# Turning softmax tiles by key blocks from the last one, a sink column, and decay terms on the row halves of the scores

## The chip, the cores and the metric

One core of a Trainium2 chip runs the whole program. The metric is device time in microseconds (us). TensorE (PE in the profile) multiplies, VectorE (DVE) and ScalarE (ACT) work on its results, GpSimd (POOL) takes elementwise work and issues some DMAs, SyncE (SP) issues the loads of weights. Each engine runs its own instructions in order, and they wait for each other on semaphores. A measurement of this kernel can tell about 0.2% from no change.

## What is computed

512 tokens of width 1024 pass through a model of two blocks. The first has two layers; each is an FFN, a mixer and another FFN. The second has a layer with differential attention, one with forgetting attention, and a convolutional FFN after each. Three kinds of stage hold attention, and each of them has eight slots, one for each pair of heads (or of softmaxes):

```
# mixer ("mix_0", "mix_1"), heads 0 to 7: window of 128 keys, and a sink in the denominator
m = max(max(s), sink);  p = exp(s - m);  denom = sum(p) + exp(sink - m);  o = (p / denom) @ v
# mixer, heads 8 to 11 (blocks) and 12 to 15 (scores of an index decide on 128 keys of a row)
# differential attention ("diff"), per head: two softmaxes over 64 channels each
attn = softmax(q1 k1 + b) - lam * softmax(q2 k2 + b);  o = attn @ v
# forgetting attention ("fox"), 16 heads: c is the running sum of the log forget gates
logits = q k / 8 + c[t] - c[s];  p = softmax(logits over s <= t);  o = p @ v
```

Everything is float32. Large products are made in three passes of TensorE with high and low parts (`h_hi`, `h_lo`, `w_hi`, `w_lo`).

## The kernel before

Tokens are split into four query tiles of 128 (i = 0 to 3) and four key blocks of 128 (b = 0 to 3). Tile i sees i + 1 blocks, or two of them for the windowed heads (`narrow`). `pair_plan` makes a plan for each pair p of heads. Its `phases` say in which of three parts of a slot the scores of a tile are made, last tile first: tile 3; then 2 and 0; then 1 (narrow: 3 and 2; then 1 and 0).

A slot is written out by hand in `pair_slots`, for each engine, and has three parts. In part `part` of slot p, TensorE makes the scores of pair p + 1 for the tiles of that phase (`pair_scores`), turns a share of the softmax tiles of pair p by transposes into two banks in turn (`pair_turn`), and then fills with a projection (`gemm_blocks`, nine matmuls of 512 columns, six in part 2). After part 2 it multiplies the turned tiles of pair p by the values (`pair_values`). VectorE does scores plus bias, with a running minimum (`pair_max`, line 1505), the reciprocal of the row sums (`pair_sums`), part of the scaling by it (line 1537), and other work between them: in the mixer rounds of a top-k (`rounds`, lines 1466 and 1467), elsewhere the low half of the next weights (line 1223). ScalarE does the exponentials (`pair_exps`, line 974), the copies of turned tiles out of the banks (`pair_turned` of ScalarE, line 993; VectorE's share is line 1550), and the high half of the next weights (line 772). GpSimd, in the mixer, makes the low half of the next weights (`low`, line 683) and then scales all tiles of the first six pairs (`pair_scale`, line 676); of the last two pairs of the mixer and of fox it scales tiles 0 and 1, and VectorE tiles 2 and 3.

What is turned together is a step: a head x of the pair and a group n of key blocks. Before the change a step with key block 0 comes first, and key block 0 is seen by every tile. So the first transposes of a head wait until all its tiles are scaled (`pn_ready` from GpSimd, `pl_ready` from VectorE), and the steps of head 0 come ahead of those of head 1.

For windowed heads the sink goes its own way: VectorE adds minimum and sink (line 1515), ScalarE takes the exponential (line 981), VectorE adds it to the row sums (line 1527) ahead of the reciprocal (line 1528).

In fox the decay is two more terms of the sum over channels. Its high and low parts, and ones, stand in four rows of `decay_q` and `decay_k` for each head, at partition 32 * (h % 4), and line 2065 adds them to the scores by a matmul of 4 rows. The scores themselves (line 2056) are matmuls of 64 rows, head 0 of a pair on rows 0 to 63 and head 1 on rows 64 to 127. GpSimd prepares both tensors and brings the rows in with 64 DMAs.

## Time and profile before

| what | value |
|---|---|
| median of 3 runs | 3302.03 us |
| lowest and highest | 3300.53 and 3302.58 us |
| profiled execution | 3302.81 us |
| its span | 3301.0 us |
| its mean granted clock of TensorE | 0.986 of 2.4 GHz |
| TensorE busy | 3190.7 us (97%) |
| VectorE, ScalarE, GpSimd busy | 1780.7, 1160.3, 548.0 us |
| stretches with attention slots | 459 to 594, 1421 to 1556, 2055 to 2190 and 2719 to 2861 us |

The profile is one execution. Times are from the start of the span. A row of the timeline has the start, the duration, the engine, the line of the kernel, the instruction, and what it writes and reads; "x6" joins six instructions. What stands in brackets is the idle time of the engine ahead of it and what ended it. Matmuls overlap, so the distance between two starts tells more than the duration.

### The profile page before, as it was taken

What the parts mean: (1) busy time and instruction counts of PE and PEld (TensorE: products, weight loads), DVE (VectorE), ACT (ScalarE), POOL (GpSimd) and SP (SyncE); (2) the same over time, 40 slices, a digit from 0 to 9 for tenths busy, and PEclk for the clock granted to TensorE, in tenths of its full rate; (3) what the DMA queues carried; (4) which work ended last, traced back from release to release, by engine and by line L of the source; (5) the groups of instructions that cost most, each with busy time, mean ns of one, the idle gap of its engine ahead of it and who ended that gap; (6) DMA issues with size and microseconds to landing.
All of it is one profiled execution on the core that took longest, in us unless ns stands there. A gap on an engine that the chain in (4) does not pass through costs nothing.

```text
span 3301.0 us, 42533 instructions
## 1 busy us (share of the span) xinstructions
PE 3190.7 (97%) x14834; PEld 2560.7 (78%) x14834; DVE 1780.7 (54%) x2737; ACT 1160.3 (35%) x1894; POOL 548.0 (17%) x506
## 2 busy tenths in 40 slices
PE   8999998999999999988999999989999999999998
PEld 7788765788888888765888877667888886688887
DVE  4434487543445344585543454557656555576474
ACT  4323235322223222344322232534324335344242
POOL 0000335300020000254100030231000432310003
PEclk9999999999999999999999999999999999999998
DMA  4355321233333333211333323112333231123332
GB/s 123 97 141 145 105 83 33 77 98 93 96 101 96 102 89 106 76 52 39 91 108 87 105 73 115 39 58 70 105 92 99 73 91 39 52 70 101 95 97 76
DMA packets 541547, 287.99 MB, mean 87 GB/s; under 512 B 14532, under 2 KB 537511, under 8 KB 541441
## 3 DMA queue, kind: packets, MB, share of 16 engines
q1 hardware_dynamic: 535936, 273.32, 28.7%
q0 software_dynamic: 5504, 13.31, 1.4%
q8 instruction: 61, 1.00, 0.1%
q14 instruction: 46, 0.37, 0.0%
HBM read 284.30 MB, written 10.02 MB: 89 GB/s over the span
## 4 chain that ended last, share of the span: by engine, by line
PE 83%; DVE 8%; POOL 4%; issue 2%; ACT 2%; DMA 0%; DVEq 0%; ACTq 0%; POOLq 0%
PE bank L1818 69%; PE bank L1832 4%; PE bank L2056 2%; PE bank L1849 2%; PE bank L1912 1%; PE bank L2097 1%; PE bank L2120 1%; POOL probs L676 1%; DVE w_lo L1223 1%; DVE norm_t L1308 1%; ACT w_hi L772 1%; POOL probs_mix L676 1%; PE bank L1890 1%; DVE score L1467 0%; POOL decay_q L741 0%
## 5 line engine op out<-in xcount | busy, mean ns | idle before, releaser
L772 ACT ACTIVATE w_hi<-w_raw 128x1024 fp32r<-128x1024 f32 (+2 forms) x477 | 533.2, 1119 | 1425.0 <-PE bank L1818 786.7
L1818 PE MATMUL bank<-h_hi,w_hi 128*128 128x512 f32 x2548 | 1000.8, 393 | 6.9 <-DVE h_lo L1248 3.8
L1818 PE MATMUL bank<-h_hi,w_lo 128*128 128x512 f32 x2548 | 992.4, 389 | 0.0
L1818 PE MATMUL bank<-h_lo,w_hi 128*128 128x512 f32 x2536 | 987.5, 389 | 0.0
L1223 DVE TENSOR_TENSOR w_lo<-w_raw,w_hi 128x1024 fp32r<-128x1024 f32 (+1 forms) x445 | 618.9, 1392 | 462.0 <-ACT w_hi L772 461.9
L1818 PEld LDWEIGHTS bank<-h_hi,w_hi 128*128 128x128 f32 x2548 | 477.8, 188 | 119.0 <-issue 14.5
L1818 PEld LDWEIGHTS bank<-h_hi,w_lo 128*128 128x128 f32 x2548 | 477.7, 187 | 101.0
L1818 PEld LDWEIGHTS bank<-h_lo,w_hi 128*128 128x128 f32 x2536 | 475.8, 188 | 100.1 <-issue 1.9
L1818 PE MATMUL bank<-act_hi,w_hi 128*128 128x512 f32 x924 | 360.6, 390 | 0.0
L1818 PE MATMUL bank<-act_lo,w_hi 128*128 128x512 f32 x924 | 360.4, 390 | 0.0
L1818 PE MATMUL bank<-act_hi,w_lo 128*128 128x512 f32 x924 | 360.3, 390 | 0.0
L1818 PEld LDWEIGHTS bank<-act_hi,w_hi 128*128 128x128 f32 x924 | 174.1, 188 | 36.6 <-issue 0.4
L1818 PEld LDWEIGHTS bank<-act_hi,w_lo 128*128 128x128 f32 x924 | 174.0, 188 | 36.3
L1818 PEld LDWEIGHTS bank<-act_lo,w_hi 128*128 128x128 f32 x924 | 174.0, 188 | 36.2
L1338 DVE SCALAR_TENSOR_TENSOR xres<-bank,xres 128x512 f32 (+1 forms) x64 | 44.2, 691 | 248.6 <-PE bank L1818 248.5
L1323 DVE TENSOR_TENSOR scaled_g<-bank,rstd 128x512 f32<-128x512 f32 x132 | 91.2, 691 | 150.6 <-PE bank L1818 145.7
L625 POOL TENSOR_TENSOR ssq<-xres 128x512 f32<-128x512 f32 x6 | 6.2, 1040 | 967.8 <-DVE xres L1338 945.8
L889 ACT ACTIVATE gated<-scaled_g 128x512 f32<-128x512 f32 x88 | 55.6, 632 | 298.3 <-DVE scaled_g L1323 298.2
L628 POOL TENSOR_TENSOR ssq<-ssq,psq 128x512 f32<-128x512 f32 x62 | 137.6, 2219 | 4.8
L1323 DVE TENSOR_TENSOR proj<-bank,rstd 128x512 f32<-128x512 f32 (+1 forms) x84 | 57.3, 686 | 109.6 <-PE bank L1818 109.2
L1379 DVE TENSOR_TENSOR prod<-gate_r,bank 128x512 f32<-128x512 f32 x88 | 60.5, 687 | 99.1 <-PE bank L1818 99.0
L683 POOL TENSOR_TENSOR w_lo<-w_raw,w_hi 128x1024 fp32r<-128x1024 f32 x32 | 77.0, 2405 | 214.0 <-ACT w_hi L772 214.0
(321 smaller groups left out, 3973.9 us busy)
## 6 DMA issues: line engine op xcount, KB each, us to landing
w_raw<-in_ffn_w_gate_dram SPq DMA_DIRECT2D x88, 512.0 KB, 3.8
w_raw<-in_ffn_w_up_dram SPq DMA_DIRECT2D x88, 512.0 KB, 3.8
w_raw<-in_ffn_w_down_dram SPq DMA_DIRECT2D x64, 704.0 KB, 4.5
w_raw<-in_ffn_w_in_dram SPq DMA_DIRECT2D x88, 512.0 KB, 3.8
w_raw<-in_ffn_w_out_dram SPq DMA_DIRECT2D x32, 704.0 KB, 4.5
w_raw<-in_w_in_dram SPq DMA_DIRECT2D x34, 512.0 KB, 3.8
w_raw<-in_a_w_qkv_dram SPq DMA_DIRECT2D x24, 512.0 KB, 3.8
w_raw<-in_w_out_dram SPq DMA_DIRECT2D x16, 512.0 KB, 3.5
```

The costliest lines, as they stand in the source:

```text
L628: add = nc.gpsimd.tensor_tensor(ssq[:, :], ssq[:, :], psq[:, :], ALU.add)
L676: ins = nc.gpsimd.tensor_scalar(tile, tile, recip[:, g % 4, i:i + 1], None, ALU.mult)
L683: nc.gpsimd.tensor_tensor(w_lo[c % 2][:, 0:KT, :], raw[c % 2][:, 0:KT, :], w_hi[c % 2][:, 0:KT, :].bitcast(f32), ALU.subtract).then_inc(lo ...
L772: nc.scalar.activation(w_hi[c % 2][:, 0:nk, 0:cols], raw[c % 2][:, 0:nk, 0:cols], ACT.Copy).then_inc(hi_ready, 1)
L889: nc.scalar.activation(gated[:, :], scaled_g[:, :], ACT.Silu).then_inc(silu_ready, 1)
L1223: nc.vector.tensor_tensor(w_lo[c % 2][:, 0:nk, 0:cols], raw[c % 2][:, 0:nk, 0:cols], w_hi[c % 2][:, 0:nk, 0:cols].bitcast(f32), ALU.subtra ...
L1323: nc.vector.tensor_tensor(dst, result(c)[rows, :], rstd[rows, :], ALU.mult).then_inc(bank_free[c % 2], 1)
L1379: nc.vector.tensor_tensor(prod[:, :], gate_r[:, :], result(at + 1)[:, :], ALU.mult).then_inc(bank_free[(c + 1) % 2], 1)
L1818: mm = nc.tensor.matmul(result(c)[0:cols, :], w[b][:, k, 0:cols], x[k], start=(k == 0 and n == 0), stop=(k == nk - 1 and n == 2))
L1832: mm = nc.tensor.matmul(bank[c % 2][:, :], w[c % 2][:, k, :], x[k], start=(k == 0 and n == 0), stop=(k == KT - 1 and n == 2))
L1849: mm = nc.tensor.matmul(result(u)[:, :], w[u % 2][:, k, :], x[k], start=(k == 0 and n == 0), stop=(k == nk - 1 and n == 2))
L2056: mm = nc.tensor.matmul(PAIR_S[x][:, at:at + w], job["q"][:, P * i:P * (i + 1)], job["k"][:, first:first + w], start=True, stop=alone)
```

## The change

- **Steps by key blocks, from the last.** Groups are now key blocks 2 and 3, then 0, then 1 (narrow: 2 and 3, then 0 and 1). Outside the differential stage both heads' steps of a group stand together, so part 0 turns group 0 of both heads, part 1 group 1, part 2 group 2. A step waits only for the tiles that it reads. In the differential stage the upper tiles are announced apart from the lower ones. The number of transposes stays the same.
- **The sink as a column.** The biased scores of windowed heads get one more column, filled with minus the sink by a copy on VectorE ahead of each `pair_max` instruction; the exponential covers it and its row sum holds the sink. Lines 1515, 981 and 1527 go.
- **Decay on the row halves.** `decay_q` now has, on the 64 rows of each half, four rows for each of the eight pairs; `decay_k` has eight copies, zero outside the four rows of their pair. The decay matmul takes the same 64 rows as the scores. GpSimd fills `decay_k` by a copy of 4096 columns where it had a memset of 2048, `decay_q` by a memset of 512 where it had 2048, makes `causal` after the gates are ready (in the place of `rms`), and issues 36 DMAs where it had 64.

The rest of the diff replaces `off(i)` by `plan["at"][i]` where softmax tiles are addressed, and removes `sinks2`, `sink_e` and their semaphores.

```diff
@@ -54,12 +54,12 @@
-            groups=[(0,), (1, 3), (2,)], turn_at={0: 0, 1: 0, 3: T - P, 2: 0},
-            slot_at={0: 0, 1: T, 3: 2 * T - P, 2: 2 * T}, spans=[(0, T), (T, T), (2 * T, 2 * P)],
+            groups=[(2, 3), (0,), (1,)], turn_at={2: 0, 3: 2 * P, 0: 0, 1: 0},
+            slot_at={2: 0, 3: 2 * P, 0: 3 * P, 1: 7 * P}, spans=[(0, 3 * P), (3 * P, T), (7 * P, 3 * P)],
...
-              groups=[(0, 2), (1, 3)], turn_at={0: 0, 2: NEAR, 1: 0, 3: NEAR},
-              slot_at={0: 0, 2: NEAR, 1: 2 * NEAR, 3: 3 * NEAR}, spans=[(0, 2 * NEAR), (2 * NEAR, 2 * NEAR - P)],
+              groups=[(2, 3), (0, 1)], turn_at={2: 0, 3: NEAR, 0: 0, 1: NEAR},
+              slot_at={2: 0, 3: NEAR, 0: 3 * P, 1: 3 * P + NEAR}, spans=[(0, 3 * P), (3 * P, 2 * NEAR)],
...
@@ -78,8 +78,11 @@
-    if stage == "diff":
+    if stage != "diff":
+        plan["steps"] = sorted(plan["steps"], key=lambda s: s[1])
+    else:
         plan["parts"] = [[0], [1], [2]]
+    plan["at"] = [0, P + 1, 3 * P + 2, 5 * P + 3] if narrow else [off(i) for i in range(NT)]
...
@@ -185,7 +188,7 @@
-                scaled_n += 1
+                scaled_n += 2
...
@@ -222,9 +225,8 @@
-        causal = put("causal", [P, T], bias_at)
-        decay_q = put("decay_q", [P, 4, T], bias_at + 4 * T, f32r)
-        decay_k = put("decay_k", [P, 4, T], bias_at + 4 * 5 * T, f32r)
+        decay_q = put("decay_q", [P, T], bias_at, f32r)
+        decay_k = put("decay_k", [P, NP, T], bias_at + 4 * T, f32r)
...
@@ -286,7 +288,10 @@
-        ssq, rms, rstd = put("ssq", [P, T]), put("rms", [P, T]), put("rstd", [P, T])
+        stat_at = [room(4 * T) for _ in range(3)]
+        ssq, rms, rstd = (put(n, [P, T], at) for n, at in zip(("ssq", "rms", "rstd"), stat_at))
+        causal = put("causal", [P, T], stat_at[1])
+        own_rows = put("own_rows", [P, 2, NP])
...
@@ -726,20 +730,30 @@
+                    chain(nc.gpsimd.memset(own_rows[:, :, :], 1.0))
+                    chain(nc.gpsimd.affine_select(out=own_rows[:, :, :], in_=own_rows[:, :, :], compare_op=ALU.is_ge, fill=0.0,
+                                                  base=0, pattern=[[-HD, 2], [-4, NP]], channel_multiplier=1))
+                    chain(nc.gpsimd.affine_select(out=own_rows[:, :, :], in_=own_rows[:, :, :], compare_op=ALU.is_ge, fill=0.0,
+                                                  base=1, pattern=[[HD, 2], [4, NP]], channel_multiplier=-1))
+                    chain(nc.gpsimd.tensor_tensor(own_rows[:, 0, :], own_rows[:, 0, :], own_rows[:, 1, :], ALU.add))
+                    chain(nc.gpsimd.tensor_copy(decay_k[:, :, :],
+                                                own_rows[:, 0, :].unsqueeze(2).broadcast_to([P, NP, T])))
+                    chain(nc.gpsimd.memset(decay_q[:, :].bitcast(f32), 1.0))
+                    pool.wait_ge(fg_ready, 1)
...
-                    chain(nc.gpsimd.memset(decay_q[:, :, :].bitcast(f32), 1.0))
-                    chain(nc.gpsimd.memset(decay_k[:, :, :].bitcast(f32), 1.0))
-                    pool.wait_ge(fg_ready, 1)
-                    for h in range(16):
-                        row, col = 32 * (h % 4), h // 4
-                        for n, part in enumerate(fparts):
-                            to, r = (decay_q, row + n) if n < 2 else (decay_k, row + n)
-                            pool.dma_start(to[r:r + 1, col, :],
-                                           part[FG_ROW + h:FG_ROW + h + 1, :]).then_inc(decay_in, 16)
+                    for n, part in enumerate(fparts[0:2]):
+                        for x in range(2):
+                            pool.dma_start(decay_q[HD * x + n:HD * x + n + 4 * NP - 3:4, :],
+                                           part[FG_ROW + x:FG_ROW + 15 + x:2, :]).then_inc(decay_in, 16)
+                    for p in range(NP):
+                        for x in range(2):
+                            for n, part in enumerate(fparts[2:4], 2):
+                                r, h = HD * x + 4 * p + n, 2 * p + x
+                                pool.dma_start(decay_k[r:r + 1, p, :],
+                                               part[FG_ROW + h:FG_ROW + h + 1, :]).then_inc(decay_in, 16)
...
@@ -968,17 +982,12 @@
-                        until = len(PLAN[stage, p - 2]["groups"]) * (1 if stage == "diff" else x + 1)
-                        act.wait_ge(pt_turned, TURNED[stage, p - 2] + until)
+                        act.wait_ge(pt_turned, TURNED[stage, p - 2] + len(PLAN[stage, p - 2]["steps"]))
                     act.wait_ge(s_biased, first + j + 1)
-                    nc.scalar.activation(ring_of(stage)[n % 4][:, off(i):off(i) + w],
-                                         BIASED2[kind(stage)][x][:, off(i):off(i) + w],
+                    cols = slice(plan["at"][i], plan["at"][i] + w + (1 if plan["narrow"] else 0))
+                    nc.scalar.activation(ring_of(stage)[n % 4][:, cols], BIASED2[kind(stage)][x][:, cols],
...
-                if plan["narrow"] and ph in plan["used"]:
-                    act.wait_ge(sinkin_ready, HA * MIX[stage] + 2 * p + ph + 1)
-                    both = sink_e[:, pair_rows(stage, p), plan["tiles"][ph]]
-                    nc.scalar.activation(both, both, ACT.Exp).then_inc(sink_ready, 1)
...
@@ -1482,8 +1491,8 @@
+                ins.then_inc(pl_ready, 1)
                 if not upper:
-                    ins.then_inc(pl_ready, 1)
...
@@ -1502,18 +1511,13 @@
-                    nc.vector.tensor_tensor_reduce(BIASED2[kind(stage)][x][:, off(i):off(i) + w], PAIR_S[x][:, at:at + w],
+                    to = plan["at"][i]
+                    if plan["narrow"]:
+                        nc.vector.tensor_copy(BIASED2[kind(stage)][x][:, to + w:to + w + 1], floor)
+                    nc.vector.tensor_tensor_reduce(BIASED2[kind(stage)][x][:, to:to + w], PAIR_S[x][:, at:at + w],
...
-            def pair_sinks(stage, p, ph):
-
-                plan = PLAN[stage, p]
-                if plan["narrow"] and ph in plan["used"]:
-                    both = (slice(0, P), pair_rows(stage, p), plan["tiles"][ph])
-                    dve.wait_ge(s_biased, NT * (JOB[stage] + 2 * p) + plan["before"][ph + 1])
-                    nc.vector.tensor_tensor(sink_e[both], nmax[both], sinks2[:, MIX[stage], 2 * p:2 * p + 2, :],
-                                            ALU.add).then_inc(sinkin_ready, 1)
...
@@ -1522,9 +1526,6 @@
-                if plan["narrow"]:
-                    dve.wait_ge(sink_ready, HA * MIX[stage] + 2 * p + ph + 1)
-                    chain(nc.vector.tensor_tensor(psum_r[both], psum_r[both], sink_e[both], ALU.add))
...
@@ -2061,10 +2059,9 @@
-                            row, col = 32 * (job["decay"] % 4), job["decay"] // 4
-                            mm = nc.tensor.matmul(PAIR_S[x][:, at:at + w], decay_q[row:row + 4, col, P * i:P * (i + 1)],
-                                                  decay_k[row:row + 4, col, 0:w], start=False, stop=True,
-                                                  tile_position=(row, 0))
+                            rows = slice(HD * x, HD * (x + 1))
+                            mm = nc.tensor.matmul(PAIR_S[x][:, at:at + w], decay_q[rows, P * i:P * (i + 1)],
+                                                  decay_k[rows, p, 0:w], start=False, stop=True)
...
@@ -2077,13 +2074,15 @@
-                    if n == 0:
-                        if stage == "diff":
-                            pe.wait_ge(pl_ready, SCALED[stage, p] + 1)
-                        else:
-                            for ready, at, key in ((pn_ready, POOLED, "pool"), (pl_ready, SCALED, "dve")):
-                                if plan[key]:
-                                    pe.wait_ge(ready, at[stage, p] + 2 * len(plan[key]) - 1 + x)
+                    if stage == "diff":
+                        pe.wait_ge(pl_ready, SCALED[stage, p] + min(n, 1) + 1)
+                    else:
+                        read = {i for b in plan["groups"][n] for i in range(b, min(b + 2, NT) if plan["narrow"] else NT)}
+                        for ready, at, key, by_pool in ((pn_ready, POOLED, "pool", True), (pl_ready, SCALED, "dve", False)):
+                            of = [u for u, ph in enumerate(plan[key])
+                                  if any(i in read and (i in plan["pool_tiles"]) == by_pool for i, _ in plan["phases"][ph])]
+                            if of:
+                                pe.wait_ge(ready, at[stage, p] + 2 * of[-1] + x + 1)
...
@@ -2278,7 +2277,7 @@
-                    pe.wait_ge(decay_in, 16 * 64)
+                    pe.wait_ge(decay_in, 16 * 36)
```

Three places in the order of instructions show what moves.

TensorE, mixer, part 0 of slot 0 (line 2056 scores, 2097 transposes, `probs_77` and `probs_78` the tiles of heads 0 and 1), before:

```order
L2056 MATMUL bank<-proj 128x256
L2056 MATMUL bank<-k_swap,proj 128x256
L2097 MATMUL bank<-ident,probs_77 128x128 [waits pn_ready]
L2097 MATMUL bank<-ident,probs_77 128x128 x6
L1832 MATMUL bank<-h_hi,w_hi_55 128x512 [waits h_ready,bank_free1,lo_ready]
```

and now (line 2096 transposes, names one lower):

```order
L2054 MATMUL bank<-k_swap,proj 128x256
L2096 MATMUL bank<-ident,probs_76 128x128 [waits pn_ready]
L2096 MATMUL bank<-ident,probs_76 128x128 x2
L2096 MATMUL bank<-ident,probs_77 128x128 [waits pn_ready]
L2096 MATMUL bank<-ident,probs_77 128x128 x2
L1830 MATMUL bank<-h_hi,w_hi_55 128x512 [waits h_ready,bank_free1,lo_ready]
```

Seven transposes of head 0 became three of head 0 and three of head 1, each three with a wait of their own.

VectorE, mixer, slot 0, part 1 (the "ISA" rows are `pair_max` and its minimum), before:

```order
L1515 TENSOR_TENSOR sink_e<-nmax,sinks_148 128x2x2 [waits s_biased,dve_step]
L1505 ISA biased,nmax<-bank,bias_win,nsinks 128x256 [waits pair_ready,p_ready]
L1505 ISA nmax 128x1
L1505 ISA biased,nmax<-bank,bias_win,nsinks 128x128 [waits pair_ready,p_ready]
L1505 ISA nmax 128x1
L1505 ISA biased_mix,nmax<-bank,bias_win,nsinks 128x256 [waits pair_ready,p_ready]
L1505 ISA nmax 128x1
L1505 ISA biased_mix,nmax<-bank,bias_win,nsinks 128x128 [waits pair_ready,p_ready]
L1505 ISA nmax 128x1
L1527 TENSOR_TENSOR psum_r<-psum_r,sink_e 128x2x2 [waits sink_ready,p_ready]
L1528 RECIPROCAL recip<-psum_r 128x2x2 [waits dve_step]
```

and now:

```order
L1517 ISA biased,nmax<-bank,bias_win,nsinks 128x256
L1517 ISA nmax 128x1
L1516 COPY biased<-nsinks 128x1 [waits pair_ready,p_ready]
L1517 ISA biased,nmax<-bank,bias_win,nsinks 128x128
L1517 ISA nmax 128x1
L1516 COPY biased_mix<-nsinks 128x1 [waits pair_ready,p_ready]
L1517 ISA biased_mix,nmax<-bank,bias_win,nsinks 128x256
L1517 ISA nmax 128x1
L1516 COPY biased_mix<-nsinks 128x1 [waits pair_ready,p_ready]
L1517 ISA biased_mix,nmax<-bank,bias_win,nsinks 128x128
L1517 ISA nmax 128x1
L1529 RECIPROCAL recip<-psum_r 128x2x2 [waits p_ready]
```

Two small operations ahead of the reciprocal went, and a copy of one column came ahead of each of the four.

TensorE, fox, slot 0, from the scores of part 1 to the transposes (`bank3` and `bank4` hold the scores of heads 0 and 1, `bank5` and `bank6` the turned tiles), before:

```order
L2056 MATMUL bank3<-proj_66 128x384
L2056 MATMUL bank4<-proj_66 128x384
L2065 MATMUL bank3<-decay_k_63,decay_q_62 128x384
L2065 MATMUL bank4<-decay_k_63,decay_q_62 128x384
L2056 MATMUL bank3<-proj_66 128x128
L2056 MATMUL bank4<-proj_66 128x128
L2065 MATMUL bank3<-decay_k_63,decay_q_62 128x128
L2065 MATMUL bank4<-decay_k_63,decay_q_62 128x128
L2097 MATMUL bank5<-ident_126,probs0_77 128x128 x2
L2097 MATMUL bank6<-ident_126,probs1_78 128x128 x4
```

and now:

```order
L2054 MATMUL bank3<-proj_65 128x384
L2054 MATMUL bank4<-proj_65 128x384
L2063 MATMUL bank3<-decay_k_62,decay_q_61 128x384
L2063 MATMUL bank4<-decay_k_62,decay_q_61 128x384
L2054 MATMUL bank3<-proj_65 128x128
L2054 MATMUL bank4<-proj_65 128x128
L2063 MATMUL bank3<-decay_k_62,decay_q_61 128x128
L2063 MATMUL bank4<-decay_k_62,decay_q_61 128x128
L2096 MATMUL bank5<-ident_127,probs0_76 128x128 x4
L2096 MATMUL bank6<-ident_127,probs1_77 128x128 x4
```

The order of scores and decays is the same; the decays take 64 rows. Part 1 turns eight tiles instead of six, part 0 six instead of eight.

## Rows read from the trace of the kernel before

**Rows 1.** Page, part 4: the chain that ended last, by engine.

```profile
PE 83%; DVE 8%; POOL 4%; issue 2%; ACT 2%; DMA 0%; DVEq 0%; ACTq 0%; POOLq 0%
```

**Rows 2.** Waits of TensorE: who for whom, us in total, times, longest.

```profile
PE bank L2097 <- POOL probs L676: 12.5, 6, 2.5
...
PE bank L2056 <- DVE pen L1469: 9.7, 2, 5.0
...
PE bank L2097 <- POOL probs_mix L676: 7.2, 5, 1.7
...
PE bank L2120 <- DVE probs_t L1550: 3.9, 7, 1.2
...
PE bank L2120 <- DVE probs_t_mix L1550: 3.7, 4, 1.2
```

**Rows 3.** Timeline, mixer 0, slot 1, of all engines by start.

```profile
492.86 0.98 PE L2097 MATMUL bank<-ident,probs_mix 128*128 128x128 f32 x7 [1.72 <-POOL probs_mix L676]
...
496.48 1.05 ACT L772 ACTIVATE w_hi<-w_raw 128x1024 fp32r<-128x1024 f32 x1
...
497.67 2.40 POOL L683 TENSOR_TENSOR w_lo<-w_raw,w_hi 128x1024 fp32r<-128x1024 f32 x1 [3.39 <-ACT w_hi L772]
...
498.34 1.76 DVE L1527 TENSOR_TENSOR psum_r<-psum_r,sink_e 128x4 f32<-128x4 f32 x1
...
500.41 6.58 POOL L676 TENSOR_SCALAR probs<-probs,recip 128x256 f32<-128x256 f32 x8 [0.34 <-DVE recip L1528]
...
502.12 0.17 DVE L1527 TENSOR_TENSOR psum_r<-psum_r,sink_e 128x4 f32<-128x4 f32 x1
...
505.56 0.98 PE L2097 MATMUL bank<-ident,probs 128*128 128x128 f32 x7 [1.70 <-POOL probs L676]
```

**Rows 4.** The same slot in the chain: start, duration, what.

```profile
500.41 5.11 POOL probs L676 x6
```

**Rows 5.** Timeline of TensorE, mixer 0: its waits in slots 4 and 5.

```profile
532.47 1.37 PE L2097 MATMUL bank<-ident,probs 128*128 128x128 f32 x8 [2.14 <-POOL probs L676]
...
559.62 1.22 PE L2056 MATMUL bank<-k_sp,proj 64*128 64x256 f32 x4 [4.76 <-DVE pen L1469]
```

**Rows 6.** Windows: stretch, busy of PE, PEld, DVE, ACT, POOL, clock.

```profile
534.00:536.00 2.00, 2.00 (x6) 1.54 (x5) 0.68 (x3) 2.00 (x6) 0.00 (x0) 0.50 0.00 0
```

**Rows 7.** Timeline of TensorE, fox, slot 2, part 1, from scores to transposes.

```profile
2774.10 0.92 PE L2056 MATMUL bank<-proj 64*128 64x384 f32 x4
2774.95 0.44 PE L2065 MATMUL bank<-decay_k,decay_q 4*128 4x384 f32 x2
2775.32 0.49 PE L2056 MATMUL bank<-proj 64*128 64x128 f32 x4
2775.74 0.32 PE L2065 MATMUL bank<-decay_k,decay_q 4*128 4x128 f32 x2
2776.00 0.88 PE L2097 MATMUL bank<-ident,probs 128*128 128x128 f32 x6
```

**Rows 8.** Timeline of TensorE, mixer 0, slot 4, part 1: scores without decay.

```profile
537.17 1.14 PE L2056 MATMUL bank<-proj 64*128 64x384 f32 x8
538.24 0.88 PE L2097 MATMUL bank<-ident,probs 128*128 128x128 f32 x6
```

**Rows 9.** Timeline, fox, slot 3: transposes, then the next weights on ScalarE and VectorE.

```profile
2771.00 1.10 PE L2097 MATMUL bank<-ident,probs 128*128 128x128 f32 x8
...
2773.61 1.04 ACT L772 ACTIVATE w_hi<-w_raw 128x1024 fp32r<-128x1024 f32 x1
...
2774.68 1.22 DVE L1223 TENSOR_TENSOR w_lo<-w_raw,w_hi 128x1024 fp32r<-128x1024 f32 x1 [1.55 <-ACT w_hi L772]
```

**Rows 10.** Timeline, start of fox: GpSimd's preparation, and TensorE's wait for it.

```profile
2629.88 0.93 DVE L1259 SCALAR_TENSOR_TENSOR h_lo<-xres,gains,h_hi 128x256 fp32r<-128x256 f32 x1 [0.30 <-ACT h_hi L811]
...
2632.46 1.80 POOL L735 MEMSET decay_k<- 128x2048 f32 x1
...
2727.39 1.13 PE L2056 MATMUL bank<-proj 64*128 64x512 f32 x4 [1.26 <-DMA decay_k<-fparts]
```

15 lines of the change are left out of this document (4 added, 11 removed).

## The prediction, made before the change was run

> **What bounds the kernel now.** The chain that ended last comes first [rows 1]: 83% of it is TensorE's own work. The change takes no matmul away, so it can win only what TensorE waits, or loses between matmuls, in the four stretches with attention slots. The waits of TensorE say for whom [rows 2]. Its transposes wait 12.5 + 7.2 = 19.7 us for GpSimd's scaling, all of it in the two mixers. Scores wait 9.7 us for `pen`, the mask that VectorE's top-k makes. The products with the values wait 3.9 + 3.7 = 7.6 us for turned tiles that VectorE copies: about 3.9 in fox (`probs_t` seven times), the rest in the mixers, 1.19 of it in slot 6 of mixer 0 (the timeline shows it, and the total is what I use).
>
> The timeline of a narrow slot shows the ring [rows 3]. Transposes start at 492.86, ScalarE copies and exponentiates and gets to `w_hi` at 496.48, GpSimd makes `w_lo` from 497.67 to 500.07, then scales from 500.41, and the next transposes start at 505.56. The ring is 12.70 us long, and TensorE idles 1.70 in it, so its own work is 11.00. The first six of eight scalings take 5.11 [rows 4], all eight 6.58, so a pair of 256 and 128 columns is 1.47; with five of 256 and one of 128 in the six, one of 256 is 0.91 and one of 128 is 0.56. Head 0 needs all six, because its first step reads key block 0.
>
> **Term 1: the steps in the mixers.** Now the first step reads tiles 3 and 2. Head 0's are scaled after two operations (1.8 us), head 1's after four (3.6). The step of head 1 begins 0.32 behind that of head 0 (three transposes at 0.107, from eight in 0.86, the distance from 2771.00 to the next matmul's start; they stand as x8 in [rows 9]). Now the ring, counted from the first transpose T: head 1's transposes end at T + 0.64; ScalarE's two copies end near T + 1.35, four exponentials take 2.0, and `w_hi` starts at T + 3.3 (before: T + 3.62). From there to GpSimd's `w_lo` are 1.19, and 2.40 for it, so scaling starts at T + 6.95, if the reciprocal is there. Head 1 may be turned at T + 6.95 + 3.7 = T + 10.6, and TensorE comes to it at T + 11.0 + 0.3. The wait is gone, with 0.7 to spare, and TensorE is the bound. In part 1 all eight scalings must be done (6.6 after their start), and TensorE is there 3.7 after T, later still than that. So slots 0 to 3 lose their whole wait.
>
> In slot 4 the tiles are wide, and GpSimd needs longer: before, 2.14 us of waiting [rows 5]. Head 1's tiles 3 and 2 stand in its first two phases, which by the same reckoning leaves 0.65 per layer. What slot 5 waited (0.3) goes into the wait for `pen`, as VectorE's rounds come no sooner. In slot -1 four new copies stand ahead of scores that TensorE waits for: 0.3 per layer. Sum: 19.7 - 2 x (0.65 + 0.33 + 0.3) = **17.1 us**. The bound above is 19.7.
>
> After the wait in slot 4 the granted clock was 0.50 for a time [rows 6], so at 1.2 of 2.4 GHz; nine matmuls took 3.4 us where they take 2.07 elsewhere, and the transposes before them 0.5 more, 1.8 us in all. Before the fall TensorE had waited 2.14; behind waits of 1.7 the clock stayed. With 0.65 left it may not fall. That is 0 to 3.6 us for both layers; I take **1.8**. The 4.76 for `pen` [rows 5] stays, and its slow stretch with it.
>
> **Term 2: the sink.** VectorE's addition at 498.34 took 1.76 us for four columns, and ended at 500.10, just behind GpSimd's `w_lo` at 500.07; the same operation at 502.12, during the scaling, took 0.17 [rows 3]. So a VectorE operation with two inputs in SBUF stood still until GpSimd's two-input one ended. It goes, and with it 0.34 ahead of the scaling (in the ring above). In its place come eight copies of one column per pair, 64 in all. No row shows one; the nearest are the small additions at 0.17, which I take as 0.1 each beyond overlap. VectorE's slot was 11.6 of 12.7 busy; less 1.7 standing still and 0.4 of small operations, plus 0.8, it is 10.4 of 11.0: hidden, with 0.6 to spare. Uncovered, it would cost 0.5 a slot, 4 us.
>
> The Trainium skill ("SBUF — State Buffer", "SBUF: two separate sides") says that VectorE and GpSimd hold a shared port pair as an exclusive lock, which VectorE needs for two SBUF inputs or for a two-port mode, and that an fp32 `tensor_copy` inside SBUF triggers that mode. By the first half the addition at 498.34 is explained, though the one at 502.12 does not fit; by the second half the new copies would stand still where the addition did. That is rival A.
>
> **Term 3: values wait in the mixers.** 3.7 us for VectorE's copies in slots 6 and 7. Now VectorE's two copies come in part 1, and part 2 is ScalarE's alone, 1.4 us of matmuls ahead of the products. But part 2's transposes need the banks that VectorE empties in part 1, behind `pair_max` and the scaling: in slot 6 I get 0.4 per layer. **2.9 us**.
>
> **Term 4: differential stage.** Part 0 turns three tiles where it turned four, part 2 three for two. VectorE's long chain starts at the scores of part 2, which come 0.107 sooner. Seven slots: **0.7 us**.
>
> **Term 5: decays in fox.** Starts lie 0.85 apart for scores of 384 columns, 0.37 for the decay, 0.42 for scores of 128, 0.26 for the decay [rows 7]. Per 128 columns that is 0.213 and 0.055, and 0.21 are fixed, each time. Scores of 384 and 128 with no decay between them take 1.07 = 4 x 0.213 + 0.21 [rows 8]: fixed only once. So the 0.21 is paid when the rows in use change, from 64 to 4 and from 4 to 64 or 128. With 64 rows for both, five of eight are left out per pair: 5 x 0.207 = 1.03, and 8.3 for eight pairs. Below it could be zero, if the change from float32 scores to the other number form of the decays costs the same; the nearest rows are those of change of rows, so I take four fifths, **6.8 us**. The columns and the number of matmuls don't change.
>
> The Trainium skill ("TensorEngine Tiling (Array Packing)", "Key Properties") says that changing the tiling mode, not just the tile, drains TensorE. [Rows 7] and [rows 8] agree with 0.21 us; a rule of that kind would give the whole 8.3.
>
> **Term 6: copies in fox.** The wait of 3.9 for VectorE's copy in part 2 goes. But VectorE copies both heads' block 0 in part 1. Counted from the transposes of part 0 [rows 9]: ScalarE now makes two copies there, so `w_hi` starts 0.3 later (2.9 for 2.6), `w_lo` ends at 5.1, `pair_max` follows until 6.6, reciprocal and scaling until 7.6, copies end at 8.2 and 8.8. TensorE, faster by its scores, wants the first bank at 8.0 and the second at 8.3. New wait: 0.5 us in six or seven slots. Sum: 3.9 - 3.0 = **0.9 us**, between 3.9 and -2.
>
> **Term 7: start of fox.** TensorE waits 1.26 for the last of 64 DMAs [rows 10]. Thirty-six, each some 0.48 us apart on GpSimd's queue, end 12 us sooner, even behind `causal`: **1.3 us**. GpSimd's copy of 4096 columns takes some 3.6 us, as two memsets of 1.80 did. It runs where VectorE's `h_lo` and `w_lo` are made, both with two SBUF inputs; `h_lo` took 0.93 at 2629.88 beside GpSimd's mask, twice its usual time. If `h_lo` gets stuck behind the copy, TensorE loses up to 3; I expect the four small operations ahead of it to let `h_lo` through. Zero, at most 3.
>
> **Sum.** 17.1 + 1.8 + 2.9 + 0.7 + 6.8 + 0.9 + 1.3 = 31.5. The profiled execution took 3302.8 (span 3301.0 and 1.8 around it): 3271.3. The median of the runs is 0.8 below that execution, so **3271**.
>
> **Rivals.**
> A. *The column copies stand still behind GpSimd's `w_lo`.* For: the 1.76 us addition. Against: one column can hardly be split over two ports, and reciprocals and top-k operations beside `w_lo` did not wait. `pair_max` of part 1 starts about with `w_lo` (T + 4.6), so it would end at T + 8.6, scaling would start at T + 8.9, and the ring would be 12.3: each narrow slot gains 0.45, not 1.7. Cost 1.25 x 6, and about 1 in the first slots: 8 us, **3279**.
> B. *The switch costs what it did*, because of the number form or because 64 rows don't help. The decay term is 0 to 2: **3277**.
> C. *VectorE is the bound.* Copies of 0.17, and waits of 1 us in fox for its copies: 3 + 3 us, **3277**.
> D. *Slower.* Each column copy waits out whatever GpSimd operation it meets, scalings too. Four copies in part 0 at 0.9 and the standstill of A make VectorE's slot 10.5 + 3.6 + 2.3 = 16.4, which is 3.7 above before, 30 us for eight slots, where terms 3 to 7 and slot 4 give 18: **3314**. It decides from slots of 15 us on. Against it is the 0.17 at 502.12, in the midst of scalings [rows 3].
>
> **How the numbers follow.** My forecast 0.58 (own range 3261 to 3276), A 0.17, B 0.08, C 0.09, A with B or C 0.04 (3285), D 0.04. A measurement tells 0.2%, 6.6 us. Only D is slower. No change (3295 and up) needs A, B and C together and a stuck `h_lo`: 0.04. So faster 0.92, same 0.04, slower 0.04. Everything at its best gives 3260, A and C together 3285: the range is 3260 to 3284.
>
> **What would show it.** Right: no wait of transposes for GpSimd in slots 0 to 3, starts of them 11.0 apart instead of 12.7; no VectorE operation of 1.8 us for a few columns; column copies under 0.15; scores and decays of part 1 in fox 1.3 us instead of 1.9, fox slots near 14.3 instead of 15.3; a wait of TensorE's transposes for VectorE's copies in fox, about 0.5. Wrong: column copies of 1 to 2 us (A, D), decays with a start 0.2 late (B), VectorE without idle time in the narrow slots (C), or TensorE waiting for `h_lo` at the start of fox.

## The result, and the profile after

| what | before | after |
|---|---|---|
| median | 3302.13 us (4 runs) | 3267.43 us (4 runs, 3266.87 to 3268.18) |
| ratio | | 0.9897 (95%: 0.9882 to 0.9912) |
| profiled execution, its span | 3302.81, 3301.0 | 3267.59, 3265.8 |
| mean granted clock | 0.986 | 0.989 |
| VectorE, ScalarE, GpSimd busy | 1780.7, 1160.3, 548.0 | 1768.4, 1158.3, 536.2 |

The change saves 34.7 us, 1.0%, where 31.5 were forecast (3271 us), and 3267.4 lies in the range of 3260 to 3284. The sum is close, but some of its terms are off in both directions.

The chain that ended last, by engine, after the change (before: [rows 1]):

```profile
PE 84%; DVE 9%; issue 3%; ACT 2%; POOL 1%; DVEq 0%; DMA 0%; ACTq 0%; POOLq 0%
```

GpSimd fell from 4% to 1%. The waits of TensorE after the change (who for whom, us in total, times, longest), to be read against [rows 2]:

```profile
PE bank L2054 <- DVE pen L1478: 10.3, 2, 5.2
PE bank L2054 <- DVE nmax L1517: 9.5, 5, 3.7
...
PE bank L2096 <- POOL probs L680: 2.5, 2, 1.3
...
PE bank L2119 <- issue: 1.3, 2, 0.6
...
PE bank L2096 <- DVE probs_t L1551: 0.8, 1, 0.8
```

Waiting for scaled tiles fell from 19.7 to 2.5 us. The products with the values (line 2119) waited 7.6 us for copies, and now 1.3, for which the profile names no releaser. Waiting for the maxima (`nmax`) rose: it was 7.2 us in all before.

To see where time went I cut each trace at the same instructions: the first product of the mixer with `ckv_n`, and the first output product of each attention stage, where TensorE waits for `w_lo`. All lengths below are differences of two such starts (us). The kernels e1 to e11 are those of the next section; two of the cut stretches outside attention, and e8 (a single execution, where three operations more cost each mixer 2 to 3 us), are left out.

| kernel | mixer 0 | mixer 1 | between them | diff | fox | start to mixer 0 | last transposes to end |
|---|---|---|---|---|---|---|---|
| before | 149.18 | 149.14 | 813.12 | 635.31 | 644.19 | 443.95 | 8.51 |
| after | 139.24 | 139.26 | 813.06 | 634.03 | 634.43 | 442.14 | 6.20 |
| e1 decays alone | 148.52 | 149.16 | 813.06 | 635.13 | 635.21 | 439.98 | 6.23 |
| e2 decays on 32 rows | 137.88 | 139.27 | 811.45 | 634.59 | 638.95 | 439.88 | 6.19 |
| e3 old sink | 141.85 | 142.84 | 811.44 | 634.68 | 634.37 | 443.87 | 6.27 |
| e4 mask later | 137.42 | 136.46 | 812.82 | 631.38 | 634.41 | 443.61 | 6.28 |
| e5 fox by heads | 139.93 | 139.32 | 813.06 | 633.84 | 634.41 | 443.83 | 6.28 |
| e6 copies swapped | 138.69 | 139.27 | 811.46 | 633.82 | 631.18 | 444.15 | 6.28 |
| e7 rounds earlier | 136.64 | 135.96 | 813.06 | 634.06 | 634.36 | 443.75 | 6.27 |
| e9 two columns | 146.08 | 146.10 | 813.02 | 633.76 | 634.50 | 442.31 | 6.19 |
| e10 slower GpSimd | 137.66 | 142.74 | 811.44 | 634.14 | 634.41 | 439.79 | 6.24 |
| e11 both | 134.33 | 133.55 | 812.91 | 632.32 | 631.05 | 443.96 | 6.22 |

Between the mixers all kernels do the same, and still lengths of 811.4 and 813.1 occur; so a stretch of one execution is known to some 1.6 us. The fox stretch repeats best: six kernels with the same fox code show 634.36 to 634.50. The attention stretches hold 19.8 (mixers), 1.3 (diff) and 9.8 us (fox), 30.9 in all. In the traces 35.2 are saved. Of the rest 1.8 lie ahead of the first mixer, where the change touches nothing and the kernels scatter from 439.8 to 444.2. The other 2.3 lie behind the last transposes, and they don't scatter: that end is 8.5 long in the one trace of the kernel before and 6.2 to 6.3 in all the others, e1 with it.

**A narrow slot after the change**, of all engines, mixer 0 (against [rows 3]):

```profile
486.23 0.87 PE L2096 MATMUL bank<-ident,probs_mix 128*128 128x128 f32 x6
...
490.73 2.41 POOL L687 TENSOR_TENSOR w_lo<-w_raw,w_hi 128x1024 fp32r<-128x1024 f32 x1 [2.01 <-ACT w_hi L786]
...
491.44 0.15 DVE L1516 COPY biased<-nsinks 128x1 f32<-128x1 f32 x1
...
492.57 0.18 DVE L1529 RECIPROCAL recip<-psum_r 128x4 f32<-128x4 f32 x1
...
493.13 5.10 POOL L680 TENSOR_SCALAR probs<-probs,recip 128x256 f32<-128x256 f32 x6
...
497.19 0.88 PE L2096 MATMUL bank<-ident,probs 128*128 128x128 f32 x6
```

(This view ends at 498; all eight scalings take 6.58, as before.) The transposes have no bracket: TensorE doesn't wait. Starts are 10.96 apart (11.0 forecast, 12.70 before). The reciprocal is done before `w_lo` ends, so scaling follows at once, where 0.34 lay between them. The copy of one column takes 0.15 in the midst of `w_lo` (490.73 to 493.13). Rival A says that it would stand still. It doesn't: 28 of the 64 copies lie wholly within a `w_lo`, and each takes 0.15 to 0.16.

**The turn into the wide slots**, from slot 3 to slot 4 of mixer 0:

```profile
512.09 2.39 POOL L687 TENSOR_TENSOR w_lo<-w_raw,w_hi 128x1024 fp32r<-128x1024 f32 x1 [1.42 <-ACT w_hi L786]
512.25 2.45 DVE L1478 TENSOR_SCALAR pen<-score 128x384 fp32r<-128x384 f32 x1
...
516.12 0.70 PE L2054 MATMUL bank<-proj 64*128 64x256 f32 x4 [0.87 <-DVE nmax L1517]
...
523.01 0.55 PE L2096 MATMUL bank<-ident,probs 128*128 128x128 f32 x3 [1.25 <-POOL probs L680]
```

The mask operation on VectorE took 2.45 us for 384 columns. In the kernel before it took 0.36, because it came at 520.66, ahead of that slot's `w_lo`. Counted from the slot's first transposes (518.28 before, 508.14 now) the mask came at 2.4 and `w_lo` at 4.2; now they come at 4.1 and 3.9. The reason is the wait that is gone: before, TensorE waited 1.71 ahead of these transposes, and VectorE, which starts its slot behind the values, was 1.95 ahead of them (516.33); now it is 0.22 ahead (507.92). The mask ends just behind `w_lo` (514.70 and 514.48). The four `nmax` of part 1 and the reciprocal stand behind it; TensorE waits 0.87 for a maximum, and then 1.25 for head 1's scaled tiles. The forecast for this place was 0.65.

**The clock.** Windows of after (busy of PE, PEld, DVE, ACT, POOL, then the granted clock): slot 4, and the stretch around the product at 548.05, which had waited 5.17 for `pen`.

```profile
523.00:525.00 2.00, 1.99 (x10) 1.71 (x11) 1.86 (x7) 1.41 (x4) 1.75 (x2) 1.00 0.00 0
548.00:550.00 2.00, 1.95 (x7) 1.33 (x8) 0.07 (x1) 0.00 (x0) 0.00 (x0) 0.50 0.00 0
552.00:554.00 2.00, 2.00 (x6) 0.53 (x6) 0.17 (x1) 0.78 (x4) 1.34 (x3) 0.50 0.00 0
```

The 1.2 GHz stretch of slot 4 [rows 6] is gone in both mixers. The one at the wait for `pen` is still there, and as long as before, but it began later. In mixer 0 before the change, 2.6 us of it were waiting and 4.3 us were work; now 0.6 us are waiting and 6.3 us, until about 554.3, are work.

**A slot of fox after the change**, TensorE in parts 1 and 2 (against [rows 7]), then VectorE's copies:

```profile
2760.76 0.92 PE L2054 MATMUL bank<-proj 64*128 64x384 f32 x4
2761.22 0.63 PE L2063 MATMUL bank<-decay_k,decay_q 64*128 64x384 f32 x2
2761.69 0.39 PE L2054 MATMUL bank<-proj 64*128 64x128 f32 x4
2761.83 0.31 PE L2063 MATMUL bank<-decay_k,decay_q 64*128 64x128 f32 x2
2762.07 0.66 PE L2096 MATMUL bank<-ident,probs 128*128 128x128 f32 x4
...
2765.51 0.47 PE L2063 MATMUL bank<-decay_k,decay_q 64*128 64x256 f32 x2
2766.06 0.52 PE L2096 MATMUL bank<-ident,probs 128*128 128x128 f32 x3
2766.66 0.52 PE L2096 MATMUL bank<-ident,probs_fox 128*128 128x128 f32 x3
...
2765.23 1.28 DVE L1551 COPY probs_t<-bank 128x512 f32<-128x512 f32 x2
```

From the scores to the transposes part 1 takes 1.31 us instead of 1.90, as forecast. Slots are 14.22 long instead of 15.3. No row here shows a wait (only in the last slot is one given, 0.75 for `probs_t`), but the two heads' transposes start 0.60 apart where three take 0.39 in part 0. The reading is that the second waits for the bank that VectorE's second copy empties at 2766.5; e6 tests it. Distances between starts tell it, brackets don't.

### The profile page after: what moved, and what is told of

Same layout as the page of the kernel before. It is cut to its first block, busy times and chain, and to the rows that moved or that the text cites. A ratio compares the mean times of both kernels' runs of the same rounds, so it can differ in the third digit from the quotient of the medians.

```text
span 3265.8 us, 42562 instructions
## 1 busy us (share of the span) xinstructions
PE 3176.6 (97%) x14834; PEld 2552.1 (78%) x14834; DVE 1768.4 (54%) x2767; ACT 1158.3 (35%) x1878; POOL 536.2 (16%) x482
## 4 chain that ended last, share of the span: by engine, by line
PE 84%; DVE 9%; issue 3%; ACT 2%; POOL 1%; DVEq 0%; DMA 0%; ACTq 0%; POOLq 0%
PE bank L1816 68%; PE bank L1830 4%; PE bank L2054 2%; PE bank L1847 2%; PE bank L2096 2%; PE bank L1910 2%; PE bank L2119 1%; DVE w_lo L1232 1%; ACT w_hi L786 1%; DVE norm_t L1317 1%; POOL probs L680 1%; DVE score L1476 1%; ACT tap_v L925 0%; PE bank L1868 0%; DVE top L1475 0%
```

## The experiments

**e1: only the decays.** The kernel before with the row halves, GpSimd's new preparation and its DMAs (the decay hunks of the diff, nothing else).

> The kernel before with the decay part of the change alone: row halves, GpSimd's new preparation, 36 DMAs. My theory: the change of rows cost 0.21 us five times per pair and is gone, 8 x 1.02 = 8.2 us, and the start of fox gains 1.3: 3302.1 - 9.5 = 3292.6 us, fox slots 15.34 - 1.02 = 14.32, with the waits of 0.47 us for VectorE's copies still there. Rival: in the changed kernel the gain in fox came from the steps too, because slots that are shorter only by their scores run into VectorE's copy in part 2; then that wait grows from 0.47 to about 1.2 and the time is near 3298.

Measured: 3289.0 us (five runs, 3283.1 to 3292.2), 0.9965 of before (0.9951 to 0.9978). In the trace fox takes 9.0 us less. Two products with the values, one slot apart:

```profile
2772.75 2.38 PE L2131 MATMUL bank<-probs_t,v_all 128*64 128x512 f32 x16 [0.46 <-DVE probs_t L1562]
...
2787.08 2.38 PE L2131 MATMUL bank<-probs_t,v_all 128*64 128x512 f32 x16 [0.46 <-DVE probs_t L1562]
```

The slot is 14.33, and the wait of 0.46 is still there. The rival, that shorter slots run into that wait, falls. Up to its first scores the fox stretch is 1.1 us shorter than before, so the decays bring 7.9 us, close to the theory's 8.2.

**e2: decays on 32 rows.**

```
-                            rows = slice(HD * x, HD * (x + 1))
+                            rows = slice(HD * x, HD * x + 32)
...
-                                                  decay_k[rows, p, 0:w], start=False, stop=True)
+                                                  decay_k[rows, p, 0:w], start=False, stop=True,
+                                                  tile_position=(HD * x, 0))
```

> The changed kernel with the decays on rows 0 to 31 and 64 to 95 alone, where all rows that are not zero lie; the result is the same. Theory: TensorE pays 0.21 us whenever the number of rows in use changes, so 64 to 32 and back costs what 64 to 4 and back did: 8 x 1.02 us back, 3275.6, and starts 0.2 us apart beyond the columns, as before. Rival: the cost belonged to the 4-row form at a partition of its own, and 32 rows inside the same half are free: 3267.4.

Measured: 3269.93 us, 0.9913 of before (0.9899 to 0.9926); fox 638.95, 4.5 longer than after the change. TensorE, part 1:

```profile
2775.12 0.92 PE L2054 MATMUL bank<-proj 64*128 64x384 f32 x4
2775.96 0.44 PE L2063 MATMUL bank<-decay_k,decay_q 32*128 32x384 f32 x2
2776.33 0.49 PE L2054 MATMUL bank<-proj 64*128 64x128 f32 x4
2776.75 0.33 PE L2063 MATMUL bank<-decay_k,decay_q 32*128 32x128 f32 x2
```

The distances 0.84, 0.37, 0.42 are those of 4 rows [rows 7]. So what is paid for is the change of rows between two matmuls, whether to 32 or to 4, and all of the 0.2 us per change was back. My number for the time was wrong all the same, 3275.6 against 3269.9: slots grew by 0.56 (to 14.78) and not by 1.02, because the waiting for copies in part 2, 0.40 per slot (e6), went in exchange: its transposes start 0.39 apart here. The two do not add up. Steps and DMAs alone bring 5.2 in fox (644.19 to 638.95), decays and DMAs alone 9.0, with 1.1 in both; together they bring 9.8 and not 13.1.

**e3: the sink's old way.** The changed kernel with the old sink path: `pair_sinks`, the exponential on ScalarE and

```
-                        nc.vector.tensor_copy(BIASED2[kind(stage)][x][:, to + w:to + w + 1], floor)
...
+                    chain(nc.vector.tensor_tensor(psum_r[both], psum_r[both], sink_e[both], ALU.add))
```

> The changed kernel with the sink's old way: two small additions per part and an exponential, no column. Its steps and decays are those of the changed kernel. My theory of the prediction: VectorE's slot of 11.6 us against TensorE's 11.0, so 0.6 us in eight slots, 3272; VectorE's idle 1.2 us per slot in the changed kernel's trace leaves 0.5 of the 1.7 us standstill, 3271. Rival: the standstill sits in GpSimd's path, the reciprocal comes later and the whole ring is back at 12.7: 8 x 1.7 = 14 us, 3281. Second rival: all of it is hidden, 3267.4.

Measured: 3274.36 us, 0.9918 of before (0.9905 to 0.9932); the mixers are 2.6 and 3.6 us longer. TensorE in mixer 0:

```profile
502.00 0.55 PE L2116 MATMUL bank<-ident,probs 128*128 128x128 f32 x3 [1.01 <-POOL probs L682]
```

VectorE's addition of four columns took 2.38 us at 495.63 there, and only then came the reciprocal (498.04) and GpSimd's scaling. So the column is worth 6 to 7 us by itself, and the steps without it would have brought as much less. The standstill accounts for it, though not in every slot. Of the eight additions ahead of a reciprocal that met a `w_lo`, three began within it and took 2.13 to 2.38. Five began 0.02 to 0.06 ahead of it and took 0.16; there the sink's other addition, which is not ahead of the reciprocal, was held (2.17). The times of the theories, 3271 to 3272 and 3281, leave it between them, nearer to the first.

**e4: the mask later.** The 384-column mask operation held back until the next rounds (`held` is a list in `topk_rounds`, which is emptied at its start):

```
-                        nc.vector.tensor_scalar(pen[:, off(t):off(t + 1)], tile, TAKEN / 2, LEFT_OUT, ALU.is_gt,
-                                                ALU.mult).then_inc(pen_ready, 1)
+                        if t == 2:
+                            held.append(penalty)
+                        else:
+                            penalty()
```

> The changed kernel with the 384-column mask operation on VectorE (pen) held back until the next rounds of the top-k, one per mixer. In the changed kernel it took 2.45 us instead of 0.36, from 512.25 to 514.70, beside GpSimd's w_lo (512.09 to 514.48), and TensorE then waited 0.87 and 1.25 us. Theory: these waits come from this standstill, and go: 3267.4 - 2 x 2.12 = 3263.2, mask operation at 0.36 to 0.8 us. Rival: GpSimd's wide scalings need that time anyway (as in the kernel before, where slot 4 waited 2.14), so only the 0.87 goes: 3265.7.

Measured: 3259.96 us, 0.9875 of before (0.986 to 0.9891), 7.5 us below the changed kernel's median. The mask took 0.35 us at 516.42. The wait for `nmax` in slot 4 is gone, and this is what is left:

```profile
523.39 0.55 PE L2106 MATMUL bank<-ident,probs 128*128 128x128 f32 x3 [0.66 <-POOL probs L680]
```

The standstill was the cause: waits fell by 0.87 + 0.59 in mixer 0, and the 0.66 left is the 0.65 that the prediction had for this place. The expectation had all 2.12 go. The mixers are 1.8 and 2.8 shorter, 4.6 in all, of which the waits are 2.9. The rest of the 7.5 us lies in stretches with the same code (diff 631.4 instead of 634.0), so it is not shown to be an effect of the edit.

**e5: fox by heads.** `plan["steps"]` is sorted in the mixers alone, and ScalarE's wait for a free buffer follows it.

> The changed kernel, fox alone with its steps by heads as before (all of head 0, then head 1); groups from the last one, decays on row halves. Theory: the steps and the decays share one wait, so fox should take what it took with the decays alone: about 635.2 us from the end of the differential stage's output to the end of fox (changed kernel 634.4), slots of 14.33 instead of 14.22, and a wait for a copy in front of the values again. Time 3267.4 + 0.8 = 3268.2. Rival: the steps alone carry the 3.9 us of waits that I gave them: 3271.

Measured: 3269.84 us, 0.9897 of before (0.9881 to 0.9914). Fox took 634.41, against 634.43 with steps by groups; slots are 14.22 and the wait in front of the values is 0.36:

```profile
2770.72 2.37 PE L2124 MATMUL bank<-probs_t,v_all 128*64 128x512 f32 x16 [0.36 <-DVE probs_t L1556]
```

So in fox the order of the steps makes no difference: the same copies of VectorE are waited for, once ahead of the values and once ahead of part 2's transposes. What little the steps bring there (635.21 in e1 to 634.4) is then left to the other half of that change, beginning with the last key blocks. The expectation was 635.2, as if that part came from the order.

**e6: copies in fox swapped.**

```
-    plan["act_groups"] = range(len(plan["groups"])) if early or stage == "diff" else (0, 2)
+    plan["act_groups"] = range(len(plan["groups"])) if early or stage == "diff" else (0, 2) if stage != "fox" else (1, 2)
```

> The changed kernel, in fox VectorE copies the turned tiles of group 0 and ScalarE those of groups 1 and 2 (before: VectorE group 1, ScalarE 0 and 2). Theory: TensorE's transposes of part 2 start 0.2 and 0.28 us late in each slot of the changed kernel, because they wait for VectorE's copies of part 1, which end at 2765.9 and 2766.5 behind pair_max, reciprocal and scaling. ScalarE is free there. Slots 14.22 to 13.75, 8 x 0.48 = 3.8 us: 3263.6. Rival: the late starts are something else than that wait (the change of rows between the decay of 64 rows and transposes of 128), and stay: 3267.4.

Measured: 3265.01 us, 0.9888 of before (0.9871 to 0.9904); fox 631.18, 3.25 shorter than after the change, with 3.8 expected. TensorE, part 2:

```profile
2763.96 0.47 PE L2063 MATMUL bank<-decay_k,decay_q 64*128 64x256 f32 x2
2764.36 0.55 PE L2096 MATMUL bank<-ident,probs 128*128 128x128 f32 x3
2764.75 0.49 PE L2096 MATMUL bank<-ident,probs_fox 128*128 128x128 f32 x3
```

The distances are 0.40 and 0.39 instead of 0.55 and 0.60. So the late starts were waits for banks, and the change of rows is not in them. Slots are 13.82 long, so the wait was 0.40 per slot.

**e7: rounds earlier.**

```
-        SLOT_ROUNDS = [18, 22, 26, 30, 34, 41, 48]
+        SLOT_ROUNDS = [18, 23, 27, 32, 37, 44, 48]
```

> The changed kernel with one row of numbers changed: the top-k rounds done by the end of each slot, 18 23 27 32 37 44 48 instead of 18 22 26 30 34 41 48. The 384-column mask operation then ends slot 2, where GpSimd's w_lo is over, and slot 5 has four rounds instead of seven. Theory: the 2.12 us in slot 4 go as in e4, and the wait for pen shrinks by three rounds of 0.98, from 5.17 to 2.2; if the clock then doesn't fall, 2.9 more. Per mixer 5.1 to 8: 3251 to 3257, I say 3255. Rival: VectorE has only 1.2 to 1.4 us free in narrow slots, a fifth round costs 1.18, and TensorE waits for its maxima instead: 3262 or more.

Measured: 3261.9 us, 0.9875 of before (0.9859 to 0.9892); mixers 2.6 and 3.3 shorter, where 5 to 8 each were expected. The time is the rival's, but not for its reason.

```profile
546.96 1.23 PE L2054 MATMUL bank<-k_sp,proj 64*128 64x256 f32 x4 [3.45 <-DVE pen L1478]
```

Narrow slots took the fifth round without a wait, so the rival's mechanism falls. `pen` came 2.7 us sooner counted from the stage's start, but TensorE, which waited 0.73 in slot 4 instead of 2.12, also got there sooner, and the clock fell here too: in mixer 0 some 6.5 us of work ran at 1.2 GHz behind a wait of 3.45.

**e8: probes beside `w_lo`.** One execution, read for its rows and not for its time. After the second maximum of part 1, one VectorE operation more: copies of 2, 8, 32 and 128 columns, a multiplication of 4 columns, an addition of one (`ident` and `ones` are constants).

> The changed kernel with one VectorE operation more in part 1 of slots 0 to 2 of each mixer, inside SBUF, at the time of GpSimd's two-input w_lo. Mixer 0: copies of 2, 8 and 32 columns; mixer 1: a copy of 128 columns, a multiplication of 4 columns by a number, an addition of two single columns. Theory from the traces: additions of two columns from SBUF stand still until w_lo ends (1.76 us), and so did the mask operation with one input and 384 columns (2.45), while the 64 one-column copies took 0.15. So the number of columns decides for operations with one input: 32 and 128 columns stand still, 2 and 8 are open; the addition stands still even with one column. Rival: copies never stand still, whatever their width.

Measured, in the order of the list:

```profile
480.51 1.84 DVE L1525 COPY probe<-ident 128x2 f32<-128x2 f32 x1
...
493.08 1.40 DVE L1525 COPY probe<-ident 128x8 f32<-128x8 f32 x1
...
505.20 1.41 DVE L1525 COPY probe<-ident 128x32 f32<-128x32 f32 x1
...
1433.63 1.92 DVE L1525 COPY probe<-ident 128x128 f32<-128x128 f32 x1
...
1446.28 1.39 DVE L1527 TENSOR_SCALAR probe<-ident 128x4 f32<-128x4 f32 x1
...
1458.38 1.38 DVE L1529 TENSOR_TENSOR probe<-ident,ones 128x1 f32<-128x1 f32 x1
```

All six ended within 0.1 us of the end of `w_lo`. The first began at 480.51 and ended at 482.35; `w_lo` ran from 479.92 to 482.32. So a copy of two columns stands still, where the sink's copies of one column do not; an addition stands still even with one.

**e9: two columns.** Rival A made real: the sink's copy writes two columns (a gap column behind each tile's sink takes the second).

```
-    plan["at"] = [0, P + 1, 3 * P + 2, 5 * P + 3] if narrow else [off(i) for i in range(NT)]
+    plan["at"] = [0, P + 2, 3 * P + 4, 5 * P + 6] if narrow else [off(i) for i in range(NT)]
...
-                        nc.vector.tensor_copy(BIASED2[kind(stage)][x][:, to + w:to + w + 1], floor)
+                        k = min(n + 2, HA) - n
+                        nc.vector.tensor_copy(BIASED2[kind(stage)][x][:, to + w:to + w + k],
+                                              nsinks[:, MIX[stage], n:n + k])
```

> The changed kernel with the copies of the sink two columns wide instead of one (a gap column behind each sink takes the second; head 7 keeps one). It is rival A of the prediction made real: in e8 a copy of 2 columns stood still until GpSimd's w_lo ended, while copies of one column took 0.15 beside it. Theory: the first copy of part 1 stands still for 2.2 us (490.97 to 493.13 in the changed kernel's times), the reciprocal comes 2.2 and the scaling 1.7 later, of which 0.7 is spare: about 1.0 to 1.3 us in three slots of each mixer, 6 to 8 us, and the prediction said 8 for rival A: 3275. Rival: a wide copy costs only what it takes, and the standstill in e8 came from its operands: 3267.4.

Measured: 3281.05 us, 0.9928 of before (0.9914 to 0.9942), 13.6 above the changed kernel; each mixer is 6.84 longer. VectorE and TensorE:

```profile
481.40 2.32 DVE L1517 COPY biased<-nsinks 128x2 f32<-128x2 f32 x1
...
489.56 0.32 DVE L1517 COPY biased<-nsinks 128x2 f32<-128x2 f32 x1
```

```profile
484.85 0.50 PE L1832 MATMUL bank<-h_hi,w_hi 128*128 128x512 f32 x1 [1.13 <-DVE nmax L1519]
...
497.80 0.50 PE L1832 MATMUL bank<-h_hi,w_hi 128*128 128x512 f32 x1 [1.71 <-DVE nmax L1519]
```

The mechanism of rival A exists, and costs 13.6 us where the prediction had put it at 8. It costs them in another place, too: in slots 1 to 3 the projection's matmuls of line 1832 wait for VectorE, which stands in front of their bank with its maxima, and TensorE waits for no scaled tile there. Only slot 0 shows the path of rival A, with 0.64 of waiting for scaled tiles. Beside GpSimd's scalings these copies took 0.16 to 0.51 us.

**e10: slower GpSimd.**

```
+                        for _ in range((2, 4)[MIX[name]] if 1 <= p < 4 else 0):
+                            chain(nc.gpsimd.tensor_scalar(probe[:, :], ident[:, :], 2.0, None, ALU.mult))
```

> The changed kernel with idle work for GpSimd between w_lo and the scaling of pairs 1 to 3: two multiplications of 128 columns (0.56 each, with the semaphores about 1.25 us) in mixer 0, four (2.5) in mixer 1. It measures what the prediction called 0.7 us to spare for head 1. Theory: in mixer 0 each of three slots waits 0.5, in mixer 1 1.8, in front of head 1's transposes: mixer stretches 139.2 to 140.8 and to 144.7, 3274. Rival: the first step of head 0 is the tight one and waits from 1.25 on as well, or GpSimd's idle 2.0 us per slot takes up both: 3267.4 to 3269.

Measured: 3269.67 us (3265.65 in the profiled execution, the lowest of four), 0.9899 of before (0.9884 to 0.9914). Two waits for scaled tiles, of mixer 0 and of mixer 1, and between them the mask and the wait for `pen`:

```profile
496.16 0.55 PE L2099 MATMUL bank<-ident,probs 128*128 128x128 f32 x3 [0.30 <-POOL probs L681]
...
510.86 0.36 DVE L1481 TENSOR_SCALAR pen<-score 128x384 fp32r<-128x384 f32 x1
...
545.41 1.18 PE L2057 MATMUL bank<-k_sp,proj 64*128 64x256 f32 x4 [5.17 <-DVE pen L1481]
...
1447.72 0.55 PE L2099 MATMUL bank<-ident,probs 128*128 128x128 f32 x3 [1.25 <-POOL probs L681]
```

Slots grew from 10.96 to 11.44 by 1.25 us of work, and to 12.65 by 2.5: 0.8 us are spare in both, where the prediction had 0.7. With 1.25 more it is head 1 that waits (0.30 in the row, 0.48 by starts), with 2.5 both (0.19 and 1.25). Mixer 0 should have grown by three times 0.48, and is 1.6 shorter than after the change. Two things are behind it. One is the clock: behind the same wait of 5.17 us it was low until about 548.5 here, for 3 us of work, and for 6 in the changed kernel, which gives 1.65. The other is slot 4. With waits back in the narrow slots the mask began at 510.86, 0.3 ahead of `w_lo` (511.18), took 0.36, and TensorE waited 0.49 in slot 4 where it had waited 2.12. Mixer 1 has the same 0.47 there, with no gain from the clock: its slots alone would have added 5.1, and it grew by 3.5. So e10 shows the standstill of e4 a second time, from the other side.

**e11: rounds and copies.** The edit is e6's swap and `SLOT_ROUNDS = [18, 23, 28, 33, 39, 45, 48]`.

> The changed kernel with e6's copies in fox and a still earlier row of rounds: 18 23 28 33 39 45 48. In e7 TensorE still waited 3.45 us for pen, and VectorE idled 1.2 to 1.9 us at the turn of each slot. With three rounds in slot 5 instead of four, and mask and rounds in slots 1 to 4 filling that idle time, pen comes two rounds earlier. Theory: wait for pen 3.45 to about 1.5, and if the clock stays, 2.9 more per mixer: mixer stretches 136.3 to about 132; fox 634.4 to 631.2: 3267.4 - 14 - 3.2 = 3250. Rival: slots 3 and 4 with six rounds make VectorE late for the wide scores, GpSimd's scaling in slot 4 comes later, and the mixers stay at 136 to 138: 3258 to 3262.

Measured: 3253.16 us, 0.985 of before (0.9836 to 0.9863), with 3250 expected: the fastest of all, 14.3 below the changed kernel.

```profile
523.85 0.55 PE L2096 MATMUL bank<-ident,probs 128*128 128x128 f32 x3 [0.57 <-POOL probs L680]
...
546.25 0.70 PE L2054 MATMUL bank<-k_sp,proj 64*128 64x256 f32 x4 [2.47 <-DVE pen L1478]
```

The wait for `pen` is 2.47 instead of 5.17, with 1.5 expected, and the clock still fell behind it.

## Why the prediction was right, and which steps were not

| term | forecast | measured |
|---|---|---|
| 1, waits in the mixers | 17.1 | about 14.3: scaled tiles 17.2 less, `nmax` 2.3 more, `pen` 0.6 more |
| 1, clock | 1.8 (0 to 3.6) | 4.1, of it 3.4 in slot 4 |
| 2, sink | hidden | hidden, 0.15 per copy; the old way costs 6 to 7 (e3) |
| 3, values in the mixers | 2.9 | 2.4 (3.7 to 1.3) |
| 4, differential stage | 0.7 | 1.3, within scatter |
| 5, decays | 6.8 (0 to 8.3) | 7.9 alone (e1) |
| 6, copies in fox | 0.9 | 0.8 (635.21 to 634.43) |
| 7, start of fox | 1.3 | 1.1: the wait of 1.26 for the DMA is gone, one of 0.39 came |
| outside attention | 0 | 4.3 in the traces |

The mixers' terms as measured give 20.8, their stretches 19.8; the difference of 1.0 is not traced.

That the sum came out this close is in part luck: the waits in the mixers were put 2.8 too high, the clock 2.3 and the decays 1.1 too low, and these cancel. The clock's 1.8 was half of a range of 0 to 3.6, not a reckoning.

**Right in mechanism and size.** The ring: TensorE is the bound of narrow slots, at 10.96 for 11.0, with 0.8 to spare for 0.7 (e10). Slot -1, the one ahead of slot 0, waits 0.24 more in each mixer for its `nmax`, where 0.3 was reckoned. The copies in fox: a wait of 3.9 goes and a new one of 0.40 per slot comes for the same two VectorE copies, at 2766.06 and 2766.66; e6 removed it and got 3.25 back. The switch: e2 shows that the change of rows costs 0.2 us. The term took four fifths of the whole 8.3 for caution with the number form, which costs nothing visible, and was 1.1 us too small. The Trainium skill ("TensorEngine Tiling (Array Packing)", "Key Properties") says that a change of tiling mode drains TensorE; a cost at 64 to 32 rows (e2) as at 64 to 4 agrees with it.

**The step that was mis-sized: slot 4.** "Leaves 0.65 per layer" took GpSimd's scaling for the only thing that can be late. It became 0.87 + 1.25, because VectorE's mask operation slid into `w_lo`. The prediction had counted VectorE's slot, and had even read from [rows 3] that such a thing happens to an addition, but had looked for it only at the operations that the change adds, not at those it moves. e4 shows the cause, and the 0.66 left there is the forecast. This one place is nearly the whole of the 2.8 us. The wait for `pen` is right in the sum, which has 0.33 each for it, though the text also says that it stays; it grew by 0.41 and 0.21.

**The clock** was mis-sized the other way. Added up over windows (busy time by one minus clock), the mixers lost 6.7 and 7.1 us before and 4.8 and 4.9 after. 1.7 in each is slot 4, whose fall is gone in both: behind 0.87 and 1.25 us of waiting it did not fall, behind 2.14 it had. The rest, 0.2 and 0.5, is the balance of more low clock behind `pen` (about 1 us) and less in slot -1, and nothing shows it to be the change's: behind the same wait of 5.17 us low stretches of some 3 and of 6 us of work occur (e10, after).

**The start of fox.** The prediction feared that `h_lo` would get stuck behind GpSimd's copy of 4096 columns. `h_lo` got through, and the first `w_lo` of VectorE behind it got stuck, for which TensorE waited:

```profile
2607.52 3.60 POOL L739 CAST decay_k<-own_rows 128x4096 fp32r<-128x4096 f32 x1
...
2612.25 0.51 PE L1816 MATMUL bank<-h_hi,w_hi 128*128 128x512 f32 x1 [0.39 <-DVE w_lo L1232]
```

**Rivals.** A fell, by a single column: e9 shows it alive with two, and dearer (13.6 for 8), since it hits TensorE's projection banks too. The Trainium skill ("SBUF — State Buffer", "SBUF: two separate sides") says that an fp32 copy inside SBUF enters the mode that needs the shared ports; from two columns on e8 and e9 agree, with one column 28 copies at 0.15 to 0.16 beside `w_lo` don't. B fell with e2 and the rows of fox. C fell: VectorE is busy 9.5 us of 10.96 in narrow slots, where 10.4 were reckoned, and in fox its copies cost 0.40 per slot, where 0.5 was reckoned. D's copies that wait for scalings exist only with two columns, and then at 0.2 to 0.5.

**Open.** The medians lie 34.7 apart and the attention stretches 30.9, so some 4 us are left that no term of the prediction has and no edit explains. The part ahead of the first mixer is within the scatter. The 2.3 at the end of the program are not: only the kernel before has them, in its one trace, and e1, which holds nothing but the decays, is already without them. Whether they belong to that part of the change or to that one execution stays open.

## To carry to other kernels

When a change moves an engine's work in time, look up in the trace where each of its operations will now meet the other engine's long two-input one; here a 0.36 us mask took 2.45, and holding it back behind the maxima made the mixers 4.6 us shorter. Two savings that end at the same wait don't add up: take the size of the second from a trace in which the first is already done. A wait can hide between back-to-back transposes without a bracket, so compare distances of starts with the same group elsewhere.

## What the runs showed of the hardware

- Beside GpSimd's two-input `w_lo` (2.40 us) VectorE's copies of 2 to 128 columns from SBUF to SBUF, multiplications of 4 and 384 columns and additions of 1 and 4 columns, once it had begun, ended only when it ended (1.38 to 2.45 us). Those that began before it, if only by 0.02 us, took their usual time: additions 0.16 (e3), the mask of 384 columns 0.36 (e10), that of 512 columns 0.43 (469.20, `w_lo` at 469.58). Copies of one column (0.15), reciprocals (0.18), `pair_max`, whose scores come from a bank, and top-k operations did not wait.
- Beside GpSimd's scalings, which have one input from SBUF and a number per row, additions of four columns took 0.16 to 0.21 in the kernel before.
- GpSimd's copy of 4096 columns (3.60 us, from 2607.52) held VectorE's `w_lo` too: 2.95 us at 2609.25 instead of 1.22. TensorE waited 0.39 for it.
- A change of rows between matmuls cost TensorE 0.2 us, from 64 to 32 (e2) as to 4 (before) and back, on top of the columns.
- Behind equal waits of 5.17 us the clock stayed at 1.2 GHz for 3 us of work in one run (e10, mixer 0) and for 6 in another (after).
